# A two-block transformer forward pass on one core: the first weight tiles loaded ahead of the input, the bias-table products placed between chunks, and weight splits issued ahead of waits at the forget gate and the output projections

## The reference, cut to what matters

```python
h = rms_norm(x, g_attn)
z = h @ w_in                      # fq fk fv f_logit nq kc vc ksl vsl kwn vwn ...
log_f = log_sigmoid(f_logit + b_f); c = cumsum(log_f)      # forget gate of 8 heads
# bias of both blocks: rel_bias_table[rel_bucket(distance)]
x = x + merged @ w_out            # output projection, block 1 (and again in block 2)
h = rms_norm(x, g_mlp); x = x + square(relu(h @ w_ff1)) @ w_ff2
...
h = h + mixed @ w_out_2           # output projection, block 2
hn = rms_norm(h, ffn_norm_g_2); h = h + (silu(hn @ w_ffn_gate) * (hn @ w_ffn_up)) @ w_ffn_down
```

## Time and profile before

| | |
|---|---|
| median of 3 runs | 1601.37 us (1600.44 to 1603.34) |
| the profiled execution, own time | 1603.95 us |
| its span on the core | 1602.1 us |
| PE busy | 1535.9 us, 96% of the span |
| DVE, ACT, POOL busy | 817.2, 617.7, 354.6 us |
| mean granted clock of PE | 0.982 |

### The profile page before, as it was taken

The page is one execution under the profiler, slowest core; times in us unless marked ns, Lnnn a source line. Parts: engine busy times, 40 slices in busy tenths (PEclk is TensorE's granted clock), DMA queues, the critical chain, the costliest instruction groups (busy, mean ns, idle before and its releaser), DMA issues.

```text
span 1602.1 us, 19523 instructions
## 1 busy us (share of the span) xinstructions
PE 1535.9 (96%) x7202; PEld 1219.5 (76%) x7202; DVE 817.2 (51%) x1644; ACT 617.7 (39%) x1118; POOL 354.6 (22%) x364
## 2 busy tenths in 40 slices
PE   6999989999999999999999999989999999999995
PEld 5787665688878888888888788755687888888884
DVE  5547566444344343433436697567364543443444
ACT  5433567423244232222446343556443322222222
POOL 3200445200020000000036534434441210120112
PEclk9999999999999999999999999989999999999998
DMA  5653200333232323233232662312422332332321
GB/s 190 126 130 106 79 1 15 118 96 102 79 101 84 97 94 100 92 103 95 93 99 67 156 177 98 104 47 66 146 86 85 98 100 92 101 97 93 104 79 54
DMA packets 46669, 154.11 MB, mean 96 GB/s; under 512 B 5698, under 2 KB 5890, under 8 KB 46576
## 3 DMA queue, kind: packets, MB, share of 16 engines
q1 hardware_dynamic: 41840, 137.63, 26.6%
q0 software_dynamic: 4736, 15.25, 4.6%
HBM read 142.78 MB, written 9.55 MB: 95 GB/s over the span
## 4 chain that ended last, share of the span: by engine, by line
PE 88%; DVE 6%; ACT 3%; issue 2%; DMA 1%; DVEq 0%; POOL 0%; SPq 0%; ACTq 0%
PE PSA L578 85%; PE PSA L780 1%; PE PSA L924 1%; ACT AR L1299 1%; DMA WR<-w_in 1%; DVE WL L1693 1%; DVE AR L1783 0%; ACT AHL L1347 0%; DVE AHL L1899 0%; DVE AR L1781 0%; DVE AR L1808 0%; DVE AR L2371 0%; DVE AR L2278 0%; ACT Bh L1378 0%; DMA AR<-AR 0%
## 5 line engine op out<-in xcount | busy, mean ns | idle before, releaser
L578 PE MATMUL PSA<-Ah,WH 128*128 128x512 f32 x1072 | 425.3, 397 | 22.8 <-DVE WL L1693 22.8
L578 PE MATMUL PSA<-Ah,WL 128*128 128x512 f32 x1072 | 420.0, 392 | 0.0
L578 PE MATMUL PSA<-Al,WH 128*128 128x512 f32 x1072 | 420.0, 392 | 0.0
L1227 ACT CAST WH<-WR 128x1024 fp32r<-128x1024 f32 (+3 forms) x234 | 240.8, 1031 | 229.4 <-PE PSA L578 215.2
L1693 DVE TENSOR_TENSOR WL<-WR,WH 128x1024 fp32r<-128x1024 f32 (+3 forms) x207 | 252.9, 1222 | 69.0 <-ACT WH L1227 68.6
L578 PEld LDWEIGHTS PSA<-Ah,WH 128*128 128x128 f32 x1072 | 203.1, 189 | 69.2 <-issue 27.6
L578 PE MATMUL PSA<-Bh,WH 128*128 128x512 f32 (+1 forms) x592 | 230.8, 390 | 5.9 <-DVE Bl L1970 4.0
L578 PEld LDWEIGHTS PSA<-Al,WH 128*128 128x128 f32 x1072 | 203.1, 189 | 42.7 <-issue 0.7
L578 PEld LDWEIGHTS PSA<-Ah,WL 128*128 128x128 f32 x1072 | 202.8, 189 | 43.0
L578 PE MATMUL PSA<-Bh,WL 128*128 128x512 f32 (+1 forms) x592 | 229.4, 388 | 0.0
L578 PE MATMUL PSA<-Bl,WH 128*128 128x512 f32 (+1 forms) x584 | 226.9, 389 | 0.0
(11 more groups left out here) (363 smaller groups left out, 1932.5 us busy)
## 6 DMA issues: line engine op xcount, KB each, us to landing
WR<-w_in SPq DMA_DIRECT2D x228, 512.0 KB, 3.5
gt_tmp<-AR SPq DMA_DIRECT2D x16, 256.0 KB, 2.2
WR<-w_in SPq DMA_DIRECT2D x8, 384.0 KB, 3.1
XT<-scr_tmp POOLq DMA_DIRECT2D x8, 264.0 KB, 13.4
XT<-xT_in SPq DMA_DIRECT2D x4, 512.0 KB, 9.0
XT<-scr_tmp POOLq DMA_DIRECT2D x8, 256.0 KB, 13.3
XT<-xT_in POOLq DMA_DIRECT2D x1, 2048.0 KB, 9.9
x_tmp<-XT POOLq DMA_DIRECT2D x1, 2048.0 KB, 7.6
```

The source lines that it names most:

```text
L578: return pe.matmul(o, l, r, start=start, stop=stop)
L1227: ac.copy(WH[p][:, 0:n], WR[j % RAW][:, 0:n]).then_inc(w_hi, 1)
```

## The change: what it does, and the diff

It loads weight tile 0 ahead of x, and x as five DMAs (one, one, two, two, two chunks), with tile 1 behind all of x. ACT runs one small Square first and splits tile 0 ahead of the first chunk of x; tiles 1, 2 and 3 come behind all of x. PE runs fq 0 and fq 1 one after the other, the sums within fq 2 ahead of its chunk 5, the products of table r within fq 3 and of table f within fk 0 (ahead of chunks 2 and 5). DVE copies GC behind fk 0's split instead of ahead of its result. At the forget gate, ACT splits kv 3 ahead of Exp and DVE splits it ahead of the wait for Ln. In both output projections DVE splits tile i+2 ahead of the wait for the result of tile i.

```diff
+X_LOADS = (0, 1), (1, 1), (2, 2), (4, 2), (6, 2)
...
-            for k in range(4):
-                sp.dma_start(x3[:, 2 * k:2 * k + 2, 0:T], d["xT"][:, 2 * k:2 * k + 2, :]).then_inc(d_x[k], 16)
-                if k < 2:
-                    weights(k)
+            weights(0)
+            for k, n in X_LOADS:
+                sp.dma_start(x3[:, k:k + n, 0:T], d["xT"][:, k:k + n, :]).then_inc(d_x[X_LOADS.index((k, n))], 16)
+            weights(1)
...
-            def feat(j, src, nk, o, ready=None, om=None):
+            def feat(j, src, nk, o, ready=None, om=None, beside=()):
                 ws = halves_ready(j)
                 for k in range(nk):
+                    if k in beside:
+                        beside[k]()
...
-            feat2(tid["fq", 0], hA, [bank(0), bank(1)], wait_norm("n1"))
-            sums("n1")
-            for i in range(2, 4):
-                feat(tid["fq", i], hA, 8, bank(i))
-            pe.wait_ge(d_tab, 48)
-            for c in range(2):
+            def table_r(c):
+                pe.wait_ge(d_tab, 48)
                 mm(bank(4 + c)[0:24, 0:336], TB, OHR[:, 336 * c:336 * c + 336], True, True).then_inc(t_mm, 1)
-            pe.wait_ge(n_v.sem, n_v.end("n1"))
-            for c in range(2):
+            def table_f(c):
+                pe.wait_ge(n_v.sem, n_v.end("n1"))
                 mm(bank(7 - c)[0:8, 0:496], TB[:, 0:8], OHF[:, 496 * c:496 * c + 496], True, True).then_inc(t_mm, 1)
+            feat(tid["fq", 0], hA, 8, bank(0), wait_norm("n1"))
+            feat(tid["fq", 1], hA, 8, bank(1))
+            feat(tid["fq", 2], hA, 8, bank(2), beside={5: lambda: sums("n1")})
+            feat(tid["fq", 3], hA, 8, bank(3), beside={2: lambda: table_r(0), 5: lambda: table_r(1)})
             for i in range(4):
                 pe.wait_ge(s_lo.sem, s_lo.at("fq", 2 * i + 1))
-                feat(tid["fk", i], hA, 8, bank(i))
+                feat(tid["fk", i], hA, 8, bank(i), beside={2: lambda: table_f(0), 5: lambda: table_f(1)} if i == 0 else ())
...
+            ac.wait_ge(k_dv.sem, k_dv.at("one"))
+            ac.activation(NS[:, 24:25], ONE[:, 0:1], ACT.Square)
+            split_to(0)
             ac.wait_ge(d_cst, 16)
             for k in range(8):
-                ac.wait_ge(d_x[k // 2], 16)
+                ac.wait_ge(d_x[max(i for i in range(len(X_LOADS)) if X_LOADS[i][0] <= k)], 16)
                 raw_high("n1", k, gv[0])
-                if k == 1:
-                    split_to(1)
-                if k in (3, 5):
-                    square("n1", k - 3)
-                    square("n1", k - 2)
-            split_to(2)
-            for k in range(4, 8):
+            split_to(1)
+            for k in range(8):
                 square("n1", k)
+                if k == 3:
+                    split_to(2)
             log_table()
             split_to(3)
...
-            split_to(tid["kv", 2])
+            split_to(tid["kv", 3])
             ac.wait_ge(g_dv.sem, g_dv.at("lf", 1))
...
                 for i in range(8):
+                    split_to(tid[wo, i] + 2)
                     result(tid[wo, i])
                     if i == 0:
                         dv.wait_ge(d_res, 16)
                     dv.tensor_tensor(x3[:, i, 0:T], bank(i % 2), x3[:, i, 0:T], ALU.add).then_inc(m_wo.sem, 1)
-                    split_to(tid[wo, i] + 2)
                     raw_low(nm, i, gain)
...
+            split_to(0)
             for k in range(8):
                 raw_low("n1", k, gv[0])
-                if k == 1:
-                    split_to(1)
-            split_to(2)
+            split_to(3)
             variance("n1")
-            split_to(3)
             newton("n1")
...
-            for c in range(2):
-                dv.wait_ge(t_mm, c + 3)
-                dv.tensor_copy(GC[:, 496 * c:496 * c + 496], bank(7 - c)[0:8, 0:496]).then_inc(t_ev, 1)
             for i in range(4):
                 result(tid["fk", i])
                 scaled(bank(i), RB["n1"])
                 split_to(tid["fk", i] + 2)
+                if i == 0:
+                    for c in range(2):
+                        dv.wait_ge(t_mm, c + 3)
+                        dv.tensor_copy(GC[:, 496 * c:496 * c + 496], bank(7 - c)[0:8, 0:496]).then_inc(t_ev, 1)
...
             dv.scalar_tensor_tensor(out=LT, in0=LF, scalar=-1.0, in1=LF, op0=ALU.mult, op1=ALU.max).then_inc(g_dv.sem, 1)
+            split_to(tid["kv", 3])
             dv.wait_ge(g_ac.sem, g_ac.at("ln", 1))
```

More of the change, by code:

```diff
@@ L278, in build @@
         d_cst, d_cs1, d_cs2 = sem("d_cst"), sem("d_cs1"), sem("d_cs2")
-        d_x = [sem(f"d_x{i}") for i in range(4)]
+        d_x = [sem(f"d_x{i}") for i in range(len(X_LOADS))]
         d_xr, d_meta, d_x2o, d_x2i = sem("d_xr"), sem("d_meta"), sem("d_x2o"), sem("d_x2i")
```

## The result

The changed kernel takes **1589.87 us** (median of 4 runs, 1587.58 to 1593.0) where the kernel before, measured beside it, takes 1602.04 (4 runs, 1600.44 to 1603.34). The ratio is 0.9927, 95% interval 0.9912 to 0.9942: 11.7 us gained by the ratio (12.2 between the two medians) of 13.4 forecast. The interval, 9.3 to 14.1 us, takes in the forecast, and the median lies inside the forecast range. The profiled execution is the slowest of the four, 1593.0 with a span of 1591.2; the profiled one of before was 1603.95, so between the two traces lie 10.95 us.

The account below looks back on a forecast made before the run. PE was taken to bound the kernel, so only its waits and slow stretches count. Opening 5.6, forget gate 1.8 and outputs 6.0 sum to 13.4 us, taking the median from 1601.37 to 1588.0; own range 1585 to 1591.5.

Parts of the forecast that it names:

- Opening: From the start to fv: PE starts at 9.2, 5.1 us earlier, and fv at 62.2 instead of 67.80, 5.6 gained.
- Rival 1: Opening gives less: tile 0 and chunk 0 land together at 8.5, PE starts at 10.8 or later; 1592.9 us, chance 0.22.
- The wait of 0.8 at fk 0: Opening: PE ends fq 3 at about 36.1, DVE's low part comes at 36.9, so fk 0 waits 0.8 us.
- DVE as pacemaker: Opening, from fk 0's wait on: DVE, not PE, sets the pace; the row copy comes at 62.1 instead of 66.28.
- a loss of 1.6: Behind the four table products the clock falls: eight matmuls' starts take 3.51 us instead of 1.82.
- Gate: Forget gate: kv 3's earlier weight load no longer runs beside kv 0's move, 3.9 to 2.1 us; 1.8 gained.
- the 124.6 and 128.3: Forget gate: kv 3 ends at 124.6, nq 0 is split at 128.3, so PE stands 3 to 4 us there.
- Outputs: Output projections: PE's waits for DVE's WL vanish, 1.2 us at wo 2, 2.4 each at f1 0 and fg 0; sum 6.0.
- nothing there waits for a fixed time: Argument against gains being lost in attention, which takes its pace from DVE and ACT.
- Rival 2: Output loop binds: PE waits for the addition if the loop exceeds 5.45 us; only 7.4 gained, 1594.0 us, chance 0.05.
- Rival 3: The edits don't reach the end, as attention takes its pace from DVE and ACT; 1600 to 1601 us, chance 0.05.
- Rival 4: Opening's clock stays low: with 67 more slow matmuls slower than before, with all 96 about 1604.8 us; chance 0.03.

Follow-up runs that it names:

- the block put back: The changed kernel with the four table products in one block ahead of fk 0 again, as before: 1592.74 us, ratio 0.993 to the kernel before.
- the better version: The changed kernel with DVE's wait for kv 0's move put behind kv 2's scaling and nq 0's split: 1588.34 us, again 1587.68.
- the three single parts: Each on the kernel before: output splits alone 1594.16 us, again 1594.94; kv 3's gate splits alone 1600.78; opening alone 1599.22.

## Why the prediction was right, and where it was off

**Opening: right in sum, wrong in two terms, and with one cause unseen.** 5.6 forecast, 5.4 in the trace (5.7 in two others with the same opening). The landings were guessed at an even 300 GB/s in order of issue; tile 0 was 1.3 earlier, chunk 1 some 1 us later than its 8.0. Rival 1 saw this for tile 0 and chunk 0, but it was chunk 1, and slack hid it. The wait of 0.8 at fk 0 did not come. From `sums` to the end of fq 3 I had 10.0 us, in which 1.83 for the sums and 7.56 for eleven chunks leave 0.6 for two table products, where four took 2.9 before; the trace has 11.05, PE asks for fk 0 at 37.20, and the low part has been there since 36.96. A term too small, and a wait forecast from it; both are the same 1.1 us, and fv does not see either. The forecast of DVE as pacemaker from there on stands: its four times agree within 0.1.
What I did not see is that "the squares come behind all of x" was itself an edit with a price. I read POOL's additions for their own duration, and not what DVE did beside them, though the row (6.43 us for four low parts, where two took 1.41 a little earlier) was in the trace before. I had assumed 0.7 apiece for the low parts of the new order and was right only because POOL was moved away.

**The clock behind the table products.** The rows that gave a loss of 1.6 (3.51 instead of 1.82) leave 1.7; the two executions of the old opening without a fall show 1.55. With the new order 0.6 was forecast for a fall, and 0.5 was measured with the block put back.

**Gate: right.** 1.8 forecast, 1.6 to 1.8 in every trace with the edit; move 2.13 for the 2.1 put down; the stall moves to nq 0. It is 2.0 there instead of 3 to 4: the 124.6 and 128.3 of the prediction leave out the 1.8 that the same paragraph takes off the move; with it they leave 1.9.

**Outputs: right.** 1.2 + 2.4 + 2.4 = 6.0 forecast, 3.55 + 2.39 = 5.94 measured. The first additions come 4.1 to 4.4 us behind one another, for a loop put at 4.4; additions stand at PE's side with over 1 us to spare.

**The missing 1.2 us.** Ratios give 11.7, 12.8 and 11.9 in three sets, each with an interval that takes in 13.4; the edited stages 13.0 to 13.3 in three traces of the changed kernel. In the traces of before and after the attentions are 1.2 and 1.0 longer. In attention 1, six executions of kernels whose gate gains have 148.7 to 149.0, two 147.8, and one (the better version's first) 154.9, with a granted clock of 0.57 to 0.75 from 180 to 210 where the changed kernel has 1.00 to 0.72; of those without that gain four have 147.4 to 148.1 and one 150.9. Attention 2, which no edit touches, goes from 341.1 to 345.8 over all fourteen executions. So the attentions vary by more than what is looked for; that they take back a part of the gain is possible and not shown, and by which mechanism stays open. The prediction's "nothing there waits for a fixed time" was too sure: the clock grants there differ from execution to execution. Part of the 1.9 us by which the median misses 1588.0 is also the base: 1602.04 beside these runs and not 1601.37.

**Rivals.** Rival 1's spread of landings occurred, without its time. Rival 2 would have shown a wait for additions; there is none. Rival 3 is excluded by the three single parts, each of which is faster than the kernel before. Rival 4 needs 67 slow matmuls; the opening has ten.

## What to carry to other kernels

When work is moved on one engine, look at how long the instructions of *other* engines take beside it, before and after: a due-time sum sees only waits, and here the main gain of the opening hung on VectorE's instructions being 0.68 instead of 1.60 us once GpSimd was quiet. A split that depends on nothing that its engine waits for belongs ahead of the wait; follow it until the next wait in the program order, since the stall moves there (kv 3 to nq 0), and hide that one too. And judge edits of 2 to 6 us by stages from start to start: two measurements of one kernel, 9.3 and 6.6 us, agreed to 0.02 in the stages that were edited.

## What was not expected of the hardware

- DVE beside POOL: low parts of 128x512 take 1.60 us beside POOL's additions and 0.68 without; a tile's low part 2.3, 1.88 or 1.53 instead of 1.23, by how far into an addition it starts. It ends 1.1 us behind the end of that addition in each of these cases.
- A move of 0.2 KB from partition to partition takes 2.1 us alone and 3.9 to 4.3 with a 512 KB load beside it.
- Of loads issued one behind another, the third (256 KB) landed 4.1 us behind the first (512 KB), and not at the pace at which bytes flowed.
- The clock falls behind products on 24 and 8 columns in most executions, but not in all: 0.51 in the kernel before, 0.54 with the gate edit alone, 0.61 with the block put back, and twice 1.00 with the same instructions.
